# Two feed-forward stages of a decoder trunk: the down projection as seven half products over 16 of its 22 k tiles

## What is computed

```python
def swiglu(h, w_gu, w_down):
    gate, up = jnp.split(h @ w_gu, 2, axis=-1)
    return (jax.nn.silu(gate) * up) @ w_down
# every layer: x = x + mixer(rms_norm(x, ...)); x = x + swiglu(rms_norm(x, g), w_gu, w_down)
```

## Time and profile before

| what | value |
|---|---|
| median of 3 runs (lowest, highest) | 2616.29 us (2615.14, 2620.3) |
| the profiled execution's own time | 2604.86 us |
| its span, first to last instruction | 2603.0 us |
| mean granted TensorE clock in it | 0.983 of full speed |
| gate/up loop of ffn0, down projection of ffn0 | 789.5 to 1261.2 us, 1261.2 to 1523.9 us |
| down projection of ffn1 | 2320.6 to 2583.2 us |
| HBM read, written | 226.51 MB, 54.06 MB |

### The profile page before, as it was taken

The page is one execution under the profiler, slowest core; times in us unless marked ns, Lnnn a source line. Parts: engine busy times, 40 slices in busy tenths (PEclk is TensorE's granted clock), DMA queues, the critical chain, the costliest instruction groups (busy, mean ns, idle before and its releaser), DMA issues. The chain is left out here.

```text
span 2603.0 us, 47342 instructions
## 1 busy us (share of the span) xinstructions
PE 2510.9 (96%) x18617; PEld 2402.5 (92%) x18648; DVE 1603.4 (62%) x2965; ACT 1056.2 (41%) x1732; POOL 108.3 (4%) x135
## 2 busy tenths in 40 slices
PE   8999988899999999999999999989999999999998
PEld 7899855577899999999999999989999999999998
DVE  6667877776557666666524566764766666663422
ACT  5567587585544222332312343553422332231201
POOL 1400133200000000000000000000000000000000
PEclk9899999999999999999999999999999999999999
DMA  6312489800123222222522213134142222261312
GB/s 207 95 41 83 137 305 392 345 31 1 34 93 106 81 84 74 74 74 74 208 83 75 92 54 123 58 95 155 62 135 74 74 74 74 74 220 40 114 49 77
DMA packets 256893, 282.59 MB, mean 109 GB/s; under 512 B 18856, under 2 KB 212650, under 8 KB 248557
## 3 DMA queue, kind: packets, MB, share of 16 engines
q1 hardware_dynamic: 244893, 205.09, 24.6%
q0 software_dynamic: 11776, 75.50, 7.7%
q10 hardware_dynamic: 80, 0.02, 0.0%
HBM read 226.51 MB, written 54.06 MB: 108 GB/s over the span
## 5 line engine op out<-in xcount | busy, mean ns | idle before, releaser
L1138 PE MATMUL ffn_acc<-trunk_x_ahead,trunk_w_hi 128*128 128x272 f32 x2464 | 470.6, 290 | 1.0 <-PEq L87 1.0
L1138 PE MATMUL ffn_acc<-ffn_x_later,ffn_w_hi_more 128*128 128x272 f32 x2112 | 396.8, 287 | 7.0 <-DVE ffn_t_u L950 3.9
L1138 PEld LDWEIGHTS ffn_acc<-trunk_x_ahead,trunk_w_hi 128*128 128x128 f32 x2464 | 389.2, 190 | 1.1 <-issue 1.1
L1138 PE MATMUL ffn_acc<-trunk_x_ahead,trunk_w_lo 128*128 128x272 f32 x1232 | 356.0, 289 | 0.0
L1188 PE MATMUL ffn_acc<-trunk_x_ahead,trunk_w_hi 128*128 128x364 f32 (+1 forms) x1344 | 346.5, 327 | 0.7 <-DVE ffn_x_later L1073 0.7
L1138 PEld LDWEIGHTS ffn_acc<-ffn_x_later,ffn_w_hi_more 128*128 128x128 f32 x2112 | 330.8, 188 | 7.9 <-issue 7.9
L1138 PE MATMUL ffn_acc<-ffn_x_later,ffn_w_lo_more 128*128 128x272 f32 x1056 | 303.8, 288 | 0.0
L1188 PE MATMUL ffn_acc<-trunk_x_ahead,trunk_w_lo 128*128 128x364 f32 (+1 forms) x768 | 251.1, 327 | 0.0
L1085 DVE TENSOR_TENSOR trunk_xT<-ffn_acc,trunk_xT 128x364 f32<-128x364 f32 x144 | 76.1, 534 | 272.3 <-PE ffn_acc L1188 272.3
L1188 PEld LDWEIGHTS ffn_acc<-trunk_x_ahead,trunk_w_hi 128*128 128x128 f32 x1344 | 239.2, 188 | 1.3 <-DVE ffn_x_later L1073 1.3
L1138 PEld LDWEIGHTS ffn_acc<-trunk_x_ahead,trunk_w_lo 128*128 128x128 f32 x1232 | 233.8, 190 | 0.0
(11 more groups left out here) (493 smaller groups left out, 5422.1 us busy)
## 6 DMA issues: line engine op xcount, KB each, us to landing
trunk_w_raw<-in_ffn_w_gu SPq DMA_DIRECT2D x88, 512.0 KB, 4.1
a_kept<-trunk_xT SPq DMA_DIRECT2D x88, 272.0 KB, 4.5
trunk_w_raw<-in_ffn_w_down SPq DMA_DIRECT2D x32, 512.0 KB, 3.7
x_saved<-trunk_xT SPq DMA_DIRECT2D x24, 544.0 KB, 2.7
trunk_x_ahead<-a_kept SPq DMA_DIRECT2D x24, 544.0 KB, 6.7
ffn_x_later<-a_kept SPq DMA_DIRECT2D x20, 544.0 KB, 7.0
trunk_w_raw<-in_sg_w_in SPq DMA_DIRECT2D x16, 512.0 KB, 4.0
attxm_w_raw<-in_att_w_in SPq DMA_DIRECT2D x14, 512.0 KB, 5.7
```

Of the source, the lines that this page charges most:

```text
L1138: last = nc.tensor.matmul(bank(2 * PAIR[p] + c)[:, 0:QC], w[:, k * P:(k + 1) * P], x(p, k)[:, c * QC:(c + 1) * QC], start=FRESH[p] and k = ...
```

## The change

Of the 22 k tiles of the down projection the first 16 are taken as 8 pairs m (k tiles 2m and 2m+1), and the product of a pair with output tiles o and o+4 is made by seven half products, as in the gate/up loop.

- The token operands of a pair (activation blocks B11, B21, B22 and the sums T1 to T4) are made in the gate/up loop, in the two sets that follow: `first_...`, `more_...` and `last_...` on ScalarE (`keep_high`, 7 copies of 544 columns a pair), VectorE (`keep_low`, 7, and `keep_sum`, 4, of 544 columns a pair) and SP (`keep`, 7 stores of 544 KB a pair, T1 in two halves) into the new DRAM tensor `o_kept` (8 pairs x 7 x 544 KB for each stage). They replace the stores of the activation tiles 0 to 15.
- Down: `FOLDED_SLABS` are 2, 3 and 3 pairs; with 4 output pairs (`FOLDED_OUTS`) that is 12 sets z. A set has seven products of 12 (first slab) or 18 matmuls of 272 columns. The 56 operand tiles are loaded back by `load_op`. For each set VectorE makes four weight sums and the low parts, ScalarE the high parts.
- A half product that goes on in the same PSUM banks waits until the one before has been read out: product 2 for product 0, 4 for 2, 5 for 3, 6 for 4. In the first slab ScalarE copies products 0, 2, 3 and 6 to `xT` and VectorE adds 1, 4 and 5; in the other slabs VectorE adds all seven. The old x isn't loaded into `xT` before; in sets 4 to 7 it comes through `back` (`load_back`) and two additions of 1088 columns (`add_back`) stand ahead of the first `d_add`.
- The last 6 k tiles stay plain (`flat`): 8 tiles q of 54 matmuls of 364 or 360 columns.

The core of the diff:

```diff
+DOWN = (B11, B21, T2, T3, T1, T4, B22)
+FOLDED = 8
+FOLDED_SLABS = ((0, 2), (2, 3), (5, 3))
+FOLDED_OUTS = (3, 2, 1, 0)
...
+            with sp.Fori(2, FOLDED) as r:
+                load_set(2 * r + 1)
+                keep_more(r - 1)
+                load_set(2 * r + 2)
+                keep_last(r - 1)
+                keep_first(r)
...
+            for z in range(SETS):
+                if z and z + 1 < SETS:
+                    load_raw0(z + 1)
+                    load_raw1(z + 1)
+                if z < 3:
+                    for i, m in slab1[5 * z:5 * z + 5]:
+                        load_op(1, i, m)
+                if z == 3:
+                    for i in DOWN:
+                        sp.wait_ge(d_products, made_at(z, i))
+                        load_op(1, i, 4)
+                    load_back(0)
...
+                if z == 7:
+                    for i in DOWN:
+                        sp.wait_ge(d_products, made_at(z, i))
+                        load_op(2, i, 6)
+                        load_op(2, i, 7)
...
+            with dve.Fori(2, FOLDED) as r:
+                finish_second(r - 1)
+                w_low(2 * r, 6, A_22, A22)
+                more_low(r - 1)
+                prepare(2 * r)
+                finish_first(r)
+                w_low(2 * r + 1, 6, A_22, A22)
+                last_low(r - 1)
+                first_low(r)
+                prepare(2 * r + 1)
...
+            for z in range(SETS):
+                more = z + 1 < SETS
+                d_low(z, D_22)
+                d_low(z, D_S4)
+                if z >= OUTS:
+                    if z < 2 * OUTS:
+                        add_back(z, 0)
+                        add_back(z, 1)
+                    d_add(z, 0)
+                d_add(z, 1)
+                if more:
+                    d_sum1(z + 1)
+                    d_sum3(z + 1)
+                if z >= OUTS:
+                    d_add(z, 2)
+                if more:
+                    d_sum2(z + 1)
+                    d_low(z + 1, D_1)
...
+            for z in range(SETS):
...
+                if copies:
+                    d_copy(z, 0)
+                if z + 1 < SETS:
+                    d_high(z + 1, D_1)
+                    if copies:
+                        d_copy(z, 2)
+                    d_high(z + 1, D_S2)
+                    if copies:
+                        d_copy(z, 3)
...
+            def folded(z, n, i):
+                pe.wait_ge(d_lo_ready, d_count(z, DOWN_NEEDS[n]))
...
+                else:
+                    pe.wait_ge(*read_of(z, {2: 0, 4: 2, 5: 3, 6: 4}[n]))
...
+            for z in range(SETS):
+                for n, i in enumerate(DOWN):
+                    folded(z, n, i)
```

More of the change, by code:

```diff
@@ new lines, in load_raw1 @@
+            def load_raw1(z):
+                if z:
+                    sp.wait_ge(d_lo_ready, d_count(z - 1, D_22))
+                else:
+                    sp.wait_ge(w_lo_ready, w_count(LAST, A_22))
+                (m0, n), o = pairs_of(z), sets[z][1]
+                for h in range(2):
+                    sp.dma_start(two_of(W.raw[:, 1, :], n * P)[:, h, :].rearrange("p (m c) -> p m c", c=P),
+                                 dn_pairs[o + KH][h][:, m0:m0 + n, :]).then_inc(d_loaded[1], 16)
@@ L716, in _ @@
+            keep_last(FOLDED - 1)
+            store_act(FLAT)
+            with sp.Fori(FLAT + 2, LAST) as r:
                 load_set(r + 1)
                 store_act(r - 1)
[L718 to L721, removed]
+            load_raw0(0)
+            load_raw1(0)
             store_act(LAST - 1)
[L723 to L726, removed]
-                load_act(j)
@@ L728, in _ @@
[L728 to L735, removed]
+            for j in range(4):
+                sp.wait_ge(stage_stored[j], 32 * FOLDED)
@@ new lines, in d_add, with add_back @@
+            def d_add(z, n):
+                dve.wait_ge(d_products, PRODUCTS * z + n + 1)
+                before = BEFORE[n]
+                dve.wait_ge(*read_of(z if before < n else z - OUTS, before))
+                if OUTS <= z < 2 * OUTS:
+                    dve.wait_ge(back_added, 2 * (z - OUTS) + 2)
+                out = target(z, n)
+                nc.vector.tensor_tensor(two(out), pair(bank_of(z, n)), two(out), ALU.add).then_inc(d_added, 1)
+            def add_back(z, h):
+                dve.wait_ge(x_back, 32 * (z - OUTS + 1))
+                for n in (1, 6) if h == 0 else (5, 4):
+                    dve.wait_ge(*read_of(z - OUTS, n))
+                out = xT[:, sets[z][1] + KH * h, :]
+                nc.vector.tensor_tensor(out, out, back[:, h, :], ALU.add).then_inc(back_added, 1)
@@ L1059, in _ @@
+            d_sum1(0)
+            d_sum3(0)
+            d_sum2(0)
+            d_sum4(0)
             make_u2(LAST)
@@ L1061, in _, with act_low @@
             make_g0(LAST)
+            d_low(0, D_1)
             make_c22(LAST)
-            def down_low(q):
-                dve.wait_ge(d_hi_ready, q + 1)
-                w = columns(q)
+            d_low(0, D_S2)
+            d_low(0, D_S3)
+            d_low(0, D_S1)
+            make_g1(LAST)
+            scale_s0(LAST)
+            finish_flat(LAST)
+            def act_low(j):
+                dve.wait_ge(a_hi_ready, j + 1)
+                hi, lo = (ops.tiles[n] for n in FLAT_TILES[j])
+                nc.vector.tensor_tensor(lo, lo.bitcast(F32), hi.bitcast(F32), ALU.subtract).then_inc(a_lo_ready, 1)
```

538 lines of the change are left out of this document (411 added, 127 removed).

## The result

The kernel after takes 2631.18 us in the median of 6 runs (2624.12 to 2632.63), the kernel before 2615.99 beside it: a ratio of 1.0054 [1.0044, 1.0065], slower by 0.54%, where 2590, and faster than before, was forecast. The profiled execution took 2632.48 us, its span is 2630.7.

A forecast was written before the change was run, and what follows sets the result against it. PE's streamed columns were taken to bound both feed-forward stages. Per stage, -23.2 + 1.1 + 4.5 + 1.3 + 1.8 + 1.4 = -13.1 us; both, -26.2, took the median 2616.3 to 2590, range 2568 to 2610.

The forecast's parts named there:

- the saving of 23.2 us a stage on PE: Down projection: matmul time falls from 262.7 to 239.5 us a stage, with 272-column matmuls at 0.125 us each.
- the late loop: Gate/up loop, rival: three stores delay the second weight load 4.1 us, costing 35 us, ending at 2625; chance 0.10.
- DVE's wait for the second weight load: Gate/up loop, in front of `sum_1`: a sign expected, the wait shrinking from 4.6 us to below 1.
- the waits in sets 0, 4 and 8: Down projection: PE waits on readers held in their queues, 1.1, 4.5 and 1.4 us a stage.
- The landing times: Down projection: loads land at S + 6.1 (set 0), S + 5.7 (set 4), S + 8.5 (set 8); S is the set's start.
- The clock: Down projection: the clock may fall after a gap; 1.3 us charged once a stage, to set 4, the longest gap.
- The rival of the clock at every wait: Down projection: six waits a stage instead of one pay 1.3 us, 13 more in all, 2603; chance 0.06.
- Set 10: Down projection: no wait charged here; outside the listed late places the layout left 0.4 us or more.
- Sets 5 to 7: Down projection: `d_add(z, 0)` ends at S + 5.0 against 4.5; 0.6 us with the wake, three times, 1.8 us.
- the dearer waits: Down projection, rival: late steps pass on; 1 us more in each of 24 sets gives 2614, half 2602; chance 0.11.
- its signs of being wrong: PE waits in the gate/up loop, clock falls in many sets, 272 columns above 0.125 us, or DVE-paced 15.7 us sets.
- The gap formula: PE matmuls: warm N / 2.4 + 2.5 ns each; by it the two stages would save 42.6 us, not 46.5.

The follow-up runs named there:

- run 11: Kernel after with six reorderings of loads and queue work, and each operand tile's load cut to its high half (output differs): 2570.50 us, 0.9828 of before.
- run 9: Kernel after with only the high halves of the operand tiles loaded, 272 KB of 544, orders unchanged (output differs): 2594.06 us, 0.9936 of before.
- run 5: Kernel after, unchanged, measured and profiled once more on another chip: 2618.92 us beside 2604.08 for the kernel before, 1.0052.
- run 4: Kernel after with the splits of two plain activation tiles moved from behind set 9's last product to places inside set 9: 2610.55 us, 1.0027 of before.
- run 8: Kernel after with six reorderings of loads, splits, additions and product readers together, no work added or removed: 2573.32 us, 0.9883 of before.

## Why the prediction was wrong

Right: the saving of 23.2 us a stage on PE (run 11 has it almost whole, at 0.125 us for a matmul of 272 columns); nothing lost in the gate/up loop, so the late loop, the rival that was to end slower, did not happen; DVE's wait for the second weight load there shrank to 0.4 us or none; 71.5 us for the plain part; 0.62 us of wait each for sets 5 to 7; and the places and mechanisms of the waits in sets 0, 4 and 8. The step that failed is the price of those waits. Four terms were wrong in size, by 20.1 us in ffn0, more than the 13.1 that were to be left:

- **The landing times** (waits 3.15, 8.48 and 4.68 us instead of 1.1, 4.5 and 1.4: 9.3 us). I had laid the streams out with 1.37 us a tile and each load behind the few that were issued just ahead. At set 0 I counted two operand tiles ahead of the weights, landing at S + 6.1; they landed at S + 8.4. Adding up what SP had asked for, less what the DMA engines had moved, 1.7 MB stood ahead, three tiles. At set 4 I put one tile ahead of x, landing at S + 5.7; 1.7 MB stood ahead, three tiles, and x landed at S + 9.6. At set 8 I had left out the weights of set 8 (0.79 MB, 2.0 us at 386 GB/s) and taken 408 GB/s for the 14 tiles (1.1 us); that is 3.1 of the 3.3 us by which the landing moved, from S + 8.5 to S + 11.8. Runs 9 and 11 show that bytes are a cause for sets 0 and 8. The Trainium skill (DMA: Bandwidth & Descriptors, Queues, rings and completion order) says that each engine takes descriptors in the order of its ring, but that a later one may finish its write before an earlier one. The trace agrees with both: the first half of x landed at 1331.7, behind the last tile asked for before it (1331.2), yet the first 192 KB of set 5's weights, asked for at 1326.0, landed at 1333.2, ahead of the second half of x (asked for at 1325.5, there at 1334.1). That a load pays for what was asked for before it is my reading of these numbers.
- **The clock** (9.3 us instead of 1.3, with the 0.23 behind each wait). I charged it once. In the profile on record it fell behind the four waits of 2.02 us and more and cost 1.8 to 3.0 us each time, more than the 1.3 that the earlier trace rows gave. The rival of the clock at every wait had 0.06; it is right for the long waits and wrong for the short ones. Over the 22 folded parts in the eleven profiles with the change, the clock fell behind all 39 waits of 3.15 us and more, behind 13 of 22 between 1.86 and 2.71, and behind none of 0.33 to 1.67. Behind the same wait of 2.0 us in set 10 it fell 9 times of 14 (run 5 has both). So how often the waits near 2 us pay could not be worked out from their length; what else decides it is open. The Trainium skill (TensorE: Matmul & The Clock Gate, A second HAM failure mode: psum-queue depth-cycling) blames, in another kernel, short idles between groups of matmuls: the 0.62 us ones of sets 5 to 7 cost no clock here (1.00 in the window behind them).
- **Set 10** (2.02 us of wait), missed. I had laid out DVE's queue for set 9 by its busy time, and not followed `act_low(0)` to ACT, where `act_high(0)` stands behind a split that needs set 9's last product (run 4).
- **Sets 5 to 7** (2.6 us instead of 1.8). The waits are as forecast; the 0.23 us behind each was not in the sum.

Of the rivals the dearer waits (0.11, 2602 to 2614) came nearest, by another way than I gave: not a little in each set, but four places with a late partner. The 0.09 for slower was nearly all the late loop's, which did not come; that the down projection alone could end slower had next to no chance in it. Of its signs of being wrong one came: the clock fell in four sets of twelve. The gap formula that the prediction sets against narrow matmuls (the Trainium skill, TensorE: Matmul & The Clock Gate, Back-to-back issue gap) is given there for an isolated matmul; in run 11's stream 1344 matmuls took 167.64 us, 0.459 ns a column, as the rows before had it.

Orders and bytes are both at work: the orders alone bring 44 us (run 8) and halved bytes alone some 30 (0.9936 against 1.0052, times 2616; run 9), both together 59 (run 11). Not tried is a change that halves the bytes and keeps the output.

## What to carry to other kernels

Before believing that a load is hidden, add up the bytes that its queue has been asked for and not yet delivered, its own included, and divide by the rate that a window shows. Worked out so, the three late loads take 4.9, 7.8 and 8.5 us (1.93 MB at 398 GB/s, 2.85 at 366, 3.29 at 386), and 5.8, 9.1 and 9.8 were measured: an estimate some 1 us short, where the prediction was short by 2.3 to 3.9. Then charge every wait of PE of 3 us and more with 1.5 to 3 us for the clock, and keep the same as a bound for waits near 2: 20 us of waiting cost 30 here. Where a change lengthens the in-order queues of several engines, follow each instruction that waits to its partner's queue: six reorderings, none of which removes work, turned 0.5% slower into 1.2% faster.

## Not expected of the hardware

- After waits of 3.15, 8.48 and 4.68 us the granted clock stood at 0.50 for the 3 us that followed and longer, 0.69 after one of 2.02, and 1.00 after the three of 0.62. The longest wait didn't cost the most: 1.8 us after 8.48, 3.0 after 3.15 (2.7 in set 0, 0.25 in set 1). Behind one and the same wait of 2.0 us it was 1.00 in one stage and 0.53 in the other (run 5).
- With the DMA engines' share at 1.03 to 1.05 the rate was 366, 386 and 398 GB/s in the windows of 8 to 22 us above, against 408 in the earlier trace rows. Weights were mixed in there, but that this is the reason isn't shown: the windows of 2 and 3 us from 1287.2 on, with weights under way too, have 411 and 396.
